# Eight of 160 dense tokens move their down products from the dense blocks to gathered rows, with the gate stage starting three blocks later

## The chip, the cores and the metric

One NeuronCore of one Trainium2 chip runs the whole program in a single launch. The metric is the device time of that launch in microseconds (us); lower is better. All arithmetic that matters here is float32. TensorE is PE in the rows (its weight loads PEld), VectorE is DVE, ScalarE is ACT, GpSimd is POOL, and SyncE is SP.

## The reference, cut to what matters

Two layers; each has a mixer (attention and pooling in layer 0, a gated MLP in layer 1) and then a PEER channel mixer, which takes most of the time. 256 tokens of width 1024 go through it. Per token, 8 heads pick 16 of 16384 one-neuron experts each, so 128 (expert, gate) pairs:

```python
expert = (i1 * PEER_N_KEYS + i2).reshape(T, PEER_HEADS * PEER_TOPK)      # ids, 128 per token
gate = jax.nn.softmax(best, axis=-1).reshape(T, PEER_HEADS * PEER_TOPK)
hid = jax.nn.gelu(jnp.einsum('cd,ckd->ck', xb, w_down[eb]))              # down products of the picked experts
out = jnp.einsum('ck,ckd->cd', (gb * hid), w_up[eb])                     # weighted sum of their up rows
```

`w_down` and `w_up` have 16384 rows of 1024 floats each, 64 MB per layer and table.

## The kernel before, in words

**Two ways of doing a token.** Tokens 0 to 63 (SPARSE) and 64 to 95 (MORE) are done by gathers: an indirect DMA from POOL fetches one row of the table for each of the 128 partitions (512 KB a gather, line 622), and DVE multiplies it with the token's activations and sums (`dots`, line 1580), or adds it with its coefficient to a running sum in the up stage (`axpy`, line 1697). There are 64 + 32 = 96 such gathers of down rows and 96 of up rows a layer. The other 160 tokens (DENSE) go through all experts: for each of 128 blocks of 128 experts, `down(b)` (line 1234) makes 8 matmuls with a 128x128 weight and the 160 token columns; `up` does the same for the up table. Each float32 matmul stands in the trace as two records, so a block has 16 records.

**Order on TensorE, per layer.** Blocks 0 to 76 of the down stage; then the transposes of gates and ids (line 1273, at block IDS_AT = 77); blocks 77 to 79; then 40 turns, each `down(G_FROM + g)` followed by `token_gates(g)` (line 1249), four one-hot matmuls (8 records) for four tokens; then 8 more down blocks; then the 128 up blocks, which begin with the pairs 0 to 7 (two blocks each). Until block G_FROM = 80 ScalarE's Gelu writes the block of activations; from there the block holds ones, gates are multiplied into it, and DVE multiplies the activated products in (`hidden`, line 1680).

**What a turn needs.** For turn g POOL builds two of the four gated one-hots (`build_first`, line 633, two instructions of line 638), DVE the compare for the other two (line 1668), and ACT scales them and builds the second factor (lines 902, 907, 910). PE waits for all three, and for the gates product of turn g-2. DVE's turn is `hidden`, `build_first`, one or two `dots`, `gate` (line 1678). POOL and ACT may run two turns ahead of PE (`g_mm`, line 635).

**POOL's queue.** It is in order. Before the turns it issues the first EARLY + RING - 1 = 49 gathers (line 641), each held until the row five earlier has landed (IN_FLIGHT, line 612) and its ring slot was read. After the build of turn g > 2 it issues what `dots_after(g + G_FROM - 2) + RING - 1` newly permits (line 648). `dots_after` spreads the rows after EARLY = 40 over 44 blocks. The first 40 dots lie between DVE's top-k steps of the second token tile (`early_dot`).

**Loads.** SP and, in part, ACT load the blocks of the tables, eight down blocks ahead; the loads from ALONE_FROM = 80 on are SP's alone. At the end of the down stage SP waits in this order (lines 560 to 565): row 90 of the ring used, load pair 2; pair 4; all rows used, load pair 3 into `spare`, where the activations of MORE lie; pair 6.

Of the kernel before, what the change touches and what calls it, by code (L numbers as in the profile page):

```python
# [15 lines left out]
P = 128  # L16
# [51 lines left out]
GATHERS = 2 * ROWS  # L68
TGROUPS = DENSE // TOK
POOL_TOK = TOK // 2  # L70
# [6 lines left out]
IDS_AT = 77  # L77
# [4 lines left out]
G_FROM = 80  # L82
# [21 lines left out]

def row_of(n):

    if SPARSE_FIRST <= n < EARLY:
        return True, n - SPARSE_FIRST
    if n >= ROWS - MORE_LAST:
        return True, n - PICKS  # L110
    return False, n if n < EARLY else n - MORE + MORE_LAST


def up_row_of(n):

    return (True, n - PICKS) if n >= PICKS else (False, n)


def token_of(g):

    return DENSE_FROM + g * TOK


def ring_uses():

    filled, last, uses = [0] * RING, [None] * RING, []
    for n in range(LAYERS * GATHERS):
        q = n % GATHERS
        slot = q % RING if q < ROWS else (q - ROWS) % UP_RING
# [73 lines left out]
def build_trunk(nc, x_d, consts_d, gfin_d, tab_d, iota_d, lncount_d, poolm_d, poolw_d,  # L203
                pscale_d, wm_d, ws_d, bs_d, cnorm_d, subk_d, wd_d, wu_d, gff_d, sel_d, rows_d, up_rows_d, out_d):
    ctx = ExitStack()
    with ctx:
# [43 lines left out]
        sel = sb("sel", [P, 4 * P + PARTS], F32)  # L250
# [27 lines left out]
        part_of = sel[:, 4 * P:]  # L278
# [66 lines left out]
        def down_psum(s):  # L345
            return ps[:, DOWN_BANKS[s], 0:DENSE]
# [59 lines left out]
        more_rows_sb, more_gates_sb = sem("more_rows_sb"), sem("more_gates_sb")  # L406
        more_ids_psum, more_found_done, more_taken = sem("more_ids_psum"), sem("more_found_done"), sem("more_taken")
# [46 lines left out]
        def _(sp):  # L454
            for l in range(LAYERS):
# [140 lines left out]
        def _(pool):  # L596
            for l in range(LAYERS):
# [10 lines left out]
                def gather(q):  # L608
# [3 lines left out]
                    if IN_FLIGHT <= q < ROWS:  # L612
                        slot, filled, _ = uses[q - IN_FLIGHT + l * GATHERS]
                        pool.wait_ge(row_full[slot], 16 * (filled + 1))
                    table = rows_d if q < ROWS else up_rows_d
                    more, j = row_of(q) if q < ROWS else up_row_of(q - ROWS)
                    if q < ROWS and more and j == 0:
                        pool.wait_ge(more_taken, l + 1)
                    if q < ROWS and not more and j % (PICKS // PIECES) == 0:
                        pool.wait_ge(picks_taken, 2 * (PIECES * l + j // (PICKS // PIECES) + 1))  # L620
                    index = (more_index if more else row_index)[:, j:j + 1]
# [41 lines left out]
        def _(act):  # L663
# [50 lines left out]
            for l in range(LAYERS):  # L714
# [140 lines left out]
                def take_hidden(b):  # L855
                    act.wait_ge(w_used, b + 1 + l * LAYER + MIX_BLOCKS)
                    nc.scalar.activation(block_of(b), down_psum(b % SLOTS), ACT.Gelu_apprx_tanh).then_inc(h_done, 1)  # L857
# [6 lines left out]
                def write_ones(i):  # L864
                    if i == 0:
                        act.wait_ge(h_rows_psum, l + 1)
                        act.wait_ge(more_rows_sb, 16 * PARTS * (l + 1))
                    first = G_FROM * DENSE + i * ONES
# [957 lines left out]
```

## Time and profile before

| | |
|---|---|
| median of three runs | 1514.79 us (1514.16 to 1517.17) |
| the profiled execution | 1503.53 us, its span 1501.7 us |
| granted TensorE clock | 0.997 of full speed |
| PE busy | 1479.2 us, 98% of the span |
| DVE, ACT, POOL busy | 892.0, 473.2, 716.5 us |
| moved by DMA | 523.12 MB, mean 348 GB/s |

The profiled execution is a single one, 11.3 us under the median of the others. A row of the timeline has the start in us, the length in us, engine, line, operation, operands and count; in brackets stands how long the engine was idle before, and what released it. Records of one engine may overlap by their latency, so the pace of a group is read from start to start.

### The profile page before, as it was taken

The page shows a single profiled execution, that of the slowest core. Times are in us where ns is not written, and L with a number is a line of the kernel's source. Part 1 is how long each engine was busy: PE and PEld are TensorE (multiplying, and loading weights), DVE is VectorE, ACT ScalarE, POOL GpSimd, SP SyncE. Part 2 cuts the span into 40 slices and gives each one's busy share as a digit, 9 for nine tenths or more (in the row PEclk, how much of TensorE's full clock was granted, in tenths as well). Part 3 has the DMA queues.
Part 4 walks back from the last instruction along what each step waited for, and adds up shares of the span by engine and source line. Part 5 has one row for each costly group of instructions (what it writes and reads, how often), then busy time and mean ns, then how long its engine had stood idle before and what let it go on. Part 6 is the DMA issues. An engine that isn't in the chain of part 4 may idle for free.

```text
span 1501.7 us, 29008 instructions
## 1 busy us (share of the span) xinstructions
PE 1479.2 (98%) x10648; PEld 1440.7 (96%) x10648; DVE 892.0 (59%) x2921; ACT 473.2 (32%) x1184; POOL 716.5 (48%) x632
## 2 busy tenths in 40 slices
PE   8999999999999999999999999999999999999996
PEld 6889999999999999999978999999999999999996
DVE  1740999948885444444623449997588834444363
ACT  6663231248881000000055533121788500000001
POOL 6577033448994333333467831333699723332350
PEclk9999999999999999999999999999999999999998
DMA  7356999999999999999845679999999999999993
GB/s 257 133 204 235 332 339 364 409 408 342 383 389 407 416 416 417 416 417 415 360 150 200 211 244 351 349 407 408 367 375 385 383 416 415 416 417 416 417 404 141
DMA packets 126416, 523.12 MB, mean 348 GB/s; under 512 B 14816, under 2 KB 15072, under 8 KB 109536
## 3 DMA queue, kind: packets, MB, share of 16 engines
q1 hardware_dynamic: 56896, 240.27, 42.0%
q0 software_dynamic: 55296, 201.35, 34.3%
q10 hardware_dynamic: 14112, 80.04, 13.1%
q8 instruction: 65, 1.06, 0.3%
q14 instruction: 47, 0.39, 0.1%
HBM read 519.48 MB, written 1.05 MB: 347 GB/s over the span
## 4 chain that ended last, share of the span: by engine, by line
PE 94%; POOL 1%; DMA 1%; issue 1%; ACT 1%; DVE 1%; DVEq 0%; POOLq 0%; SPq 0%; ACTq 0%
PE ps L992 93%; POOL w_lo L605 1%; DMA spare<-in_wu 1%; PE ps L1000 1%; ACT hT_hi L707 0%; DMA raw<-in_wm 0%; DMA xs<-in_x 0%; ACT w_hi L692 0%; ACT arena L680 0%; DVE arena L1385 0%; DVE rtmp L1374 0%; DVE arena L1523 0%; POOL arena L630 0%; PE ps L1322 0%; PE ps L1120 0%
## 5 line engine op out<-in xcount | busy, mean ns | idle before, releaser
L992 PE MATMUL ps<-arena,raw 128*128 128x160 f32 (+1 forms) x2688 | 377.4, 299 | 0.2
L992 PE MATMUL ps<-arena,w_raw 128*128 128x160 f32 (+1 forms) x2688 | 377.3, 299 | 0.0
L992 PEld LDWEIGHTS ps<-arena,raw 128*128 128x128 f32 x2688 | 368.1, 190 | 0.7 <-issue 0.7
L992 PEld LDWEIGHTS ps<-arena,w_raw 128*128 128x128 f32 x2688 | 368.2, 190 | 0.0
L622 POOL DMA_INDIRECT arena<-in_up_rows,ret x192 | 188.1, 979 | 355.1 <-DVE oh_buf L1697 263.3
L622 POOL DMA_INDIRECT arena<-in_rows,ret x192 | 200.0, 1042 | 285.8 <-ACT ret L879 104.5
L1697 DVE SCALAR_TENSOR_TENSOR oh_buf<-arena,ret,oh_buf 128x1024 f32<-128x1024 f32 x126 | 161.8, 1284 | 227.9 <-DMA arena<-in_up_rows,ret 227.9
L605 POOL TENSOR_TENSOR w_lo<-raw,w_hi 128x1024 fp32r<-128x1024 f32 x80 | 194.0, 2436 | 90.8 <-PE ps L992 66.1
L992 PE MATMUL ps<-arena 128*128 128x160 f32 (+5 forms) x1336 | 184.5, 302 | 0.4 <-DMA spare<-in_wu 0.3
L992 PEld LDWEIGHTS ps<-arena 128*128 128x128 f32 (+2 forms) x1336 | 177.9, 189 | 4.0 <-issue 2.6
L1580 DVE SCALAR_TENSOR_TENSOR arena<-arena,ps 128x1024 f32<-128x1024 f32 x128 | 153.6, 1213 | 0.0
L969 ACT ACTIVATE arena<-consts 128x768 f32<-128x768 f32 x2 | 1.7, 842 | 450.0 <-PE ps L992 450.0
L638 POOL TENSOR_SCALAR oh_buf<-iota,ret 128x128 f32<-128x128 f32 x160 | 127.0, 802 | 12.7 <-PE ps L992 10.0
L857 ACT ACTIVATE arena<-ps 128x160 f32<-128x160 f32 x160 | 48.6, 304 | 265.9 <-PE ps L992 265.9
L1697 DVE SCALAR_TENSOR_TENSOR ret<-arena,ret 128x1024 f32<-128x1024 f32 x62 | 82.6, 1333 | 69.2 <-DMA arena<-in_up_rows,ret 66.3
L692 ACT ACTIVATE w_hi<-raw 128x1024 fp32r<-128x1024 f32 x80 | 83.5, 1059 | 83.4 <-DMA raw<-in_wm 57.9
L902 ACT ACTIVATE ret<-iota,ret 128x128 f32<-128x128 f32 x320 | 100.8, 386 | 1.4 <-PE ps L992 1.4
L1633 DVE SCALAR_TENSOR_TENSOR arena<-iota,ret,ps 128x54 f32<-128x54 f32 x512 | 99.9, 265 | 0.0
L1580 DVE SCALAR_TENSOR_TENSOR arena<-arena,spare 128x1024 f32<-128x1024 f32 x64 | 76.4, 1217 | 18.5 <-DMA arena<-in_rows,ret 18.5
L1678 DVE TENSOR_TENSOR arena<-arena,ps 128x512 f32<-128x512 f32 x80 | 54.8, 685 | 52.1 <-PE ps L992 52.1
L992 PE MATMUL ps<-oh_buf,ret 128*128 128x128 f32 x640 | 84.6, 275 | 0.6 <-issue 0.6
L992 PE MATMUL ps<-arena,spare 128*128 (+1 forms) x576 | 82.2, 299 | 0.0
(149 smaller groups left out, 1780.6 us busy)
## 6 DMA issues: line engine op xcount, KB each, us to landing
raw<-in_wd SPq DMA_DIRECT2D x92, 512.0 KB, 6.8
w_raw<-in_wd SPq DMA_DIRECT2D x92, 512.0 KB, 7.6
raw<-in_wm SPq DMA_DIRECT2D x80, 512.0 KB, 3.4
low_rows<-in_wu SPq DMA_DIRECT2D x18, 1024.0 KB, 7.9
arena<-in_wu SPq DMA_DIRECT2D x18, 1024.0 KB, 7.9
arena<-in_wd SPq DMA_DIRECT2D x32, 512.0 KB, 4.9
raw<-in_wu SPq DMA_DIRECT2D x14, 1024.0 KB, 8.0
raw<-in_wu ACTq DMA_DIRECT2D x14, 1024.0 KB, 8.0
```

Of the source, the lines that this page charges most:

```text
L605: nc.gpsimd.tensor_tensor(w_lo[:, s % WLO, :], raw[:, s, :], whs[:, s].bitcast(F32), ALU.subtract).then_inc(wlo_pool, 1)
L622: nc.gpsimd.indirect_dma_start(ring[s], None, table, bass.IndirectOffsetOnAxis(ap=index, axis=0)).then_inc(row_full[s], 16)
L638: nc.gpsimd.tensor_scalar(oh1g[:, g % 2, k, :], iota[:, :], i1T[:, t:t + 1], gT[:, t:t + 1], ALU.is_equal, ALU.mult).then_inc(oh1_pool, 1)
L692: nc.scalar.activation(whs[:, s], raw[:, s, :], ACT.Copy).then_inc(whi_done, 1)
L857: nc.scalar.activation(block_of(b), down_psum(b % SLOTS), ACT.Gelu_apprx_tanh).then_inc(h_done, 1)
L902: nc.scalar.activation(oh2[:, g % 2, k, :], iota[:, :], ACT.Abs, scale=-1.0, bias=i2T[:, t:t + 1]).then_inc(oh2_far, 1)
L992: return nc.tensor.matmul(out, lhsT, rhs, start=start, stop=stop, skip_group_check=shared)
L1000: last = nc.tensor.transpose(ps[:, bank + banks[i], o:o + P], src[:, t, c * P:(c + 1) * P], ident[:, :])
L1580: nc.vector.scalar_tensor_tensor(row, row, 1.0, more_rows if more else h_rows, ALU.mult, ALU.mult, accum_out=(more_hid if more else row_hi ...
L1633: step(nc.vector.scalar_tensor_tensor(found[:, (j * 8 + k) % 24, :], places, cif[:, t, n:n + 1], pay[:, h, :], ALU.is_equal, ALU.mult, acc ...
L1678: nc.vector.tensor_tensor(part, part, gates, ALU.mult).then_inc(gmul_done, 1)
L1697: ins = nc.vector.scalar_tensor_tensor(out, row, coef[:, j:j + 1], out, ALU.mult, ALU.add)
```

## The change

MID = 8: the dense tokens 96 to 103 take their down products from eight more gathers a layer (128 partitions = 8 tokens x 16 parts, each with 8 experts), and `down` multiplies 152 columns instead of 160. The up stage keeps its 160 columns: the eight tokens' activations are multiplied into their gates before these are built into one-hots. Their turns are put last (turns 38 and 39), and there the gates product is a copy. IDS_AT goes from 77 to 80 and G_FROM from 80 to 83; there are still 40 turns, and five down blocks after them. The eight rows are rows 44 to 51 of now 104, and the rows after the fortieth are spread over 43 blocks. The row's product has its activations in `spare[:, 1]`, loaded by 16 more small DMAs of SP.

```diff
+MID, MID_TO = 8, DENSE_FROM + 8
+MID_PARTS = P // MID
+DOWN_ROWS = ROWS + MID
+GATHERS = DOWN_ROWS + ROWS
+DOWN_COLS = DENSE - MID
-IDS_AT = 77
+IDS_AT = 80
-G_FROM = 80
+G_FROM = 83
+DOT_BLOCKS = BLOCKS - G_FROM - 2
+MID_FIRST = EARLY + 4
+MID_GELU_AT, MID_SPREAD, MID_TURN = G_FROM + 14, 16, 18
 def dots_after(b):
-    return EARLY + max(0, min(ROWS - EARLY, (b - G_FROM - 1) * (ROWS - EARLY) // 44))
+    return EARLY + max(0, min(DOWN_ROWS - EARLY, (b - G_FROM - 1) * (DOWN_ROWS - EARLY) // DOT_BLOCKS))
...
+                for i in range(MID_PARTS):
+                    sp.dma_start(mid_rows[i * MID:(i + 1) * MID, :],
+                                 gff[DENSE_FROM:MID_TO, :]).then_inc(mid_rows_sb, 16)
...
-                sp.wait_ge(row_used, l * GATHERS + ROWS - ROWS % RING)
+                sp.wait_ge(row_used, l * GATHERS + DOWN_ROWS - DOWN_ROWS % RING)
                 load_up(RING_PAIR, RING_PAIR)
                 load_first(RAW_PAIRS)
-                sp.wait_ge(row_used, l * GATHERS + ROWS)
+                sp.wait_ge(row_used, l * GATHERS + DOWN_ROWS)
+                sp.wait_ge(mid_psum, l + 1)
                 load_up(SPARE_PAIR, SPARE_PAIR)
...
+                    if g == MID_GROUP:
+                        pool.wait_ge(mid_gates_done, l + 1)
...
-                        free = min(ROWS, dots_after(g + G_FROM - 2) + RING - 1)
+                        free = min(DOWN_ROWS, dots_after(g + G_FROM - 2) + RING - 1)
...
+                def activate_mid():
+                    act.wait_ge(row_used, l * GATHERS + MID_FIRST + MID)
+                    nc.scalar.activation(mid_hid, mid_hid, ACT.Gelu_apprx_tanh).then_inc(mid_gelu_done, 1)
...
+                    if with_mid:
+                        pe.wait_ge(mid_spread_done, l + 1)
+                        mm(mid_psum_of(slot), mid_rows[:, 0:P], mid_token).then_inc(mid_psum, 1)
                     out = down_psum(slot)
                     for c in range(DC):
-                        last = mm(out, block_in[:, c * P:(c + 1) * P], hT[:, c, :], c == 0, c == DC - 1)
+                        last = mm(out, block_in[:, c * P:(c + 1) * P], hT[:, c, MID:], c == 0, c == DC - 1)
...
+                pe.wait_ge(mid_of_done, l + 1)
+                mm(ps[:, 5, SEQ:SEQ + P], mid_of, idf[:, 0, :]).then_inc(more_ids_psum, 1)
...
                         nc.vector.scalar_tensor_tensor(
-                            row, row, 1.0, more_rows if more else h_rows, ALU.mult, ALU.mult,
-                            accum_out=(more_hid if more else row_hid)[:, j:j + 1]).then_inc(row_used, 1)
+                            row, row, 1.0, (h_rows, more_rows, mid_rows)[kind], ALU.mult, ALU.mult,
+                            accum_out=(row_hid, more_hid, mid_hid)[kind][:, j:j + 1]).then_inc(row_used, 1)
...
-                step(nc.vector.tensor_copy(gT, ps[:, 5, 0:SEQ]))
+                step(nc.vector.tensor_copy(gT[:, DENSE_FROM:], ps[:, 5, DENSE_FROM:SEQ]))
...
+                    if g < MID_GROUP:
+                        nc.vector.tensor_tensor(part, part, gates, ALU.mult).then_inc(gmul_done, 1)
+                    else:
+                        nc.vector.tensor_copy(part, gates).then_inc(gmul_done, 1)
+
+                def spread_mid():
+                    dve.wait_ge(mid_gelu_done, l + 1)
+                    nc.vector.tensor_tensor(mid_spread, mid_hid.unsqueeze(1).to_broadcast([P, MID_PARTS, MID]),
+                                            mid_part_of.unsqueeze(2).to_broadcast([P, MID_PARTS, MID]),
+                                            ALU.mult).then_inc(mid_spread_done, 1)
+
+                def gate_mid():
+                    b = G_FROM + MID_TURN
+                    dve.wait_ge(h_psum, b - G_FROM + 1 + hiddens_before)
+                    dve.wait_ge(mid_psum, l + 1)
+                    part = gT[:, DENSE_FROM:MID_TO]
+                    nc.vector.tensor_tensor(part, part, mid_psum_of(b % SLOTS), ALU.mult).then_inc(mid_gates_done, 1)
```

## Rows read from the trace of the kernel before

**Rows 1.** The page's part 4, chain by line; part 5, one group of weight loads.
```profile
PE 94%; POOL 1%; DMA 1%; issue 1%; ACT 1%; DVE 1%; DVEq 0%; POOLq 0%; SPq 0%; ACTq 0%
...
L992 PEld LDWEIGHTS ps<-arena,w_raw 128*128 128x128 f32 x2688 | 368.2, 190 | 0.0
```

**Rows 2.** Timeline of PE: a turn of the gate stage, and blocks before up.
```profile
382.01 1.05 PE L992 MATMUL ps<-oh_buf,ret 128*128 128x128 f32 x8
382.90 2.34 PE L992 MATMUL ps<-arena,raw 128*128 128x160 f32 x16
...
1196.70 8.86 PE L992 MATMUL ps<-arena,w_raw 128*128 128x160 f32 x64
1205.39 4.51 PE L992 MATMUL ps<-arena,low_rows 128*128 128x160 f32 x32
```

**Rows 3.** Timeline of POOL in the gate stage of layer 0.
```profile
349.43 1.59 POOL L638 TENSOR_SCALAR oh_buf<-iota,ret 128x128 f32<-128x128 f32 x2 [0.29 <-PE ps L992]
351.19 1.03 POOL L622 DMA_INDIRECT arena<-in_rows,ret  x1 [0.17 <-DVE arena L1580]
352.52 0.94 POOL L622 DMA_INDIRECT arena<-in_rows,ret  x1 [0.30 <-issue]
353.50 1.59 POOL L638 TENSOR_SCALAR oh_buf<-iota,ret 128x128 f32<-128x128 f32 x2
...
356.33 1.59 POOL L638 TENSOR_SCALAR oh_buf<-iota,ret 128x128 f32<-128x128 f32 x2
```

**Rows 4.** Timeline of PE, turn 37 of layer 0.
```profile
447.07 1.13 PE L992 MATMUL ps<-oh_buf,ret 128*128 128x128 f32 x8 [0.28 <-issue]
```

**Rows 5.** Timeline of DVE, a turn with one dot.
```profile
380.03 0.69 DVE L1678 TENSOR_TENSOR arena<-arena,ps 128x512 f32<-128x512 f32 x1 [0.67 <-PE ps L992]
380.64 1.21 DVE L1580 SCALAR_TENSOR_TENSOR arena<-arena,ps 128x1024 f32<-128x1024 f32 x1
...
381.78 0.31 DVE L1684 TENSOR_TENSOR arena<-arena,ps 128x160 f32<-128x160 f32 x1
...
383.10 0.69 DVE L1678 TENSOR_TENSOR arena<-arena,ps 128x512 f32<-128x512 f32 x1 [0.68 <-PE ps L992]
```

**Rows 6.** Timeline of POOL, layer 0: gathers number 26, 44 and 48.
```profile
258.33 0.94 POOL L622 DMA_INDIRECT arena<-in_rows,ret  x1 [1.00 <-DMA arena<-in_rows,ret]
...
317.62 1.30 POOL L622 DMA_INDIRECT arena<-in_rows,ret  x1 [1.55 <-DMA arena<-in_rows,ret]
...
...
328.50 0.94 POOL L622 DMA_INDIRECT arena<-in_rows,ret  x1 [1.61 <-DMA arena<-in_rows,ret]
```

**Rows 7.** Busy time by window; after the engines: clock, DMA share, GB/s.
```profile
270.00:300.00 30.00, 30.00 (x223) 30.00 (x222) 28.45 (x177) 6.83 (x16) 11.76 (x10) 1.00 1.03 409
390.00:420.00 30.00, 30.00 (x238) 30.00 (x237) 26.04 (x54) 25.71 (x81) 27.41 (x32) 1.00 1.00 379
```

**Rows 8.** Timeline of DVE, layer 0: end of top-k, first copy of the gates.
```profile
318.59 0.29 DVE L1647 TENSOR_TENSOR ret<-ret,gsum 128x128 f32<-128x128 f32 x1
324.45 0.42 DVE L1651 COPY ret<-ps 128x256 f32<-128x256 f32 x1 [5.56 <-PE ps L1278]
```

**Rows 9.** Timelines of POOL and DVE near the end of layer 0.
```profile
130.36 2.40 POOL L605 TENSOR_TENSOR w_lo<-raw,w_hi 128x1024 fp32r<-128x1024 f32 x1 [0.48 <-PE ps L992]
...
735.21 5.65 POOL L605 TENSOR_TENSOR w_lo<-raw,w_hi 128x1024 fp32r<-128x1024 f32 x2 [5.60 <-PE ps L992]
...
736.25 7.08 DVE L1697 SCALAR_TENSOR_TENSOR ret<-arena,ret 128x1024 f32<-128x1024 f32 x3 [2.44 <-DMA arena<-in_up_rows,ret]
```

**Rows 10.** SP's timeline, layer 1; issues of 1199 to 1202 (us to landing last).
```profile
1200.31 0.33 SPq L536 DMA_DIRECT2D spare<-in_wu  x1
...
spare<-in_wu SPq DMA_DIRECT2D x1, 1024.0 KB, 10.1
```

**Rows 11.** Timelines of DVE and PE at the end of layer 0.
```profile
747.63 1.28 DVE L1697 SCALAR_TENSOR_TENSOR ret<-arena,ret 128x1024 f32<-128x1024 f32 x1 [0.89 <-DMA arena<-in_up_rows,ret]
...
752.81 1.02 PE L992 MATMUL ps<-oh_buf,sel 128*128 128x512 f32 x2
```

More of the change, by code:

```diff
@@ L92, with column_of @@
 EARLY, EARLY_PLACES = SPARSE_FIRST + MORE - MORE_LAST, 14
+DOT_BLOCKS = BLOCKS - G_FROM - 2
+MID_FIRST = EARLY + 4
+MID_GELU_AT, MID_SPREAD, MID_TURN = G_FROM + 14, 16, 18
 def dots_after(b):
-    return EARLY + max(0, min(ROWS - EARLY, (b - G_FROM - 1) * (ROWS - EARLY) // 44))
+    return EARLY + max(0, min(DOWN_ROWS - EARLY, (b - G_FROM - 1) * (DOWN_ROWS - EARLY) // DOT_BLOCKS))
 def early_after(i):
     return (i + 1) * EARLY // EARLY_PLACES
+ROW, MORE_ROW, MID_ROW = range(3)
 def row_of(n):
[L107 to L111, printed above, removed]
+    if n < SPARSE_FIRST:
+        return ROW, n
+    if n < EARLY:
+        return MORE_ROW, n - SPARSE_FIRST
+    if MID_FIRST <= n < MID_FIRST + MID:
+        return MID_ROW, n - MID_FIRST
+    if n >= DOWN_ROWS - MORE_LAST:
+        return MORE_ROW, n - DOWN_ROWS + MORE
+    return ROW, n - MORE + MORE_LAST - (MID if n >= MID_FIRST else 0)
 def up_row_of(n):
-    return (True, n - PICKS) if n >= PICKS else (False, n)
+    return (MORE_ROW, n - PICKS) if n >= PICKS else (ROW, n)
+def column_of(g):
+    return (MID + g * TOK) % DENSE
 def token_of(g):
-    return DENSE_FROM + g * TOK
+    return DENSE_FROM + column_of(g)
 def ring_uses():
@@ L128, in ring_uses @@
         q = n % GATHERS
-        slot = q % RING if q < ROWS else (q - ROWS) % UP_RING
+        slot = q % RING if q < DOWN_ROWS else (q - DOWN_ROWS) % UP_RING
         uses.append((slot, filled[slot], last[slot]))
@@ L317, in build_trunk @@
         more_found = ret[:, 0:MORE]
+        mid_found = ret[:, MORE:MORE + MID]
+        mid_index = ret[:, MORE + MID:MORE + 2 * MID].bitcast(U32)
+        mid_hid = ret[:, MORE + 2 * MID:MORE + 3 * MID]
+        mid_rows = spare[:, 1, :]
+        mid_spread = mid_rows[:, 0:P].rearrange("p (b j) -> p b j", j=MID)
         spread = ret[:, 2 * SEQ:2 * SEQ + P].rearrange("p (b j) -> p b j", j=MORE)
+        mid_of = ret[:, 2 * SEQ + P:3 * SEQ]
+        mid_ids = mid_of.rearrange("p (b j) -> p b j", j=MID)
         h_rows = ps[:, 2:4, :].rearrange("p b n -> p (b n)")
@@ L611, in gather @@
                         pool.wait_ge(row_used, last + 1)
[L612 removed]
+                    if IN_FLIGHT <= q < DOWN_ROWS:
                         slot, filled, _ = uses[q - IN_FLIGHT + l * GATHERS]
                         pool.wait_ge(row_full[slot], 16 * (filled + 1))
[L615 to L617 removed]
+                    table = rows_d if q < DOWN_ROWS else up_rows_d
+                    kind, j = row_of(q) if q < DOWN_ROWS else up_row_of(q - DOWN_ROWS)
+                    if q < DOWN_ROWS and kind == MORE_ROW and j == 0:
                         pool.wait_ge(more_taken, l + 1)
[L619 removed]
+                    if kind == MID_ROW and j == 0:
+                        pool.wait_ge(mid_taken, l + 1)
+                    if q < DOWN_ROWS and kind == ROW and j % (PICKS // PIECES) == 0:
                         pool.wait_ge(picks_taken, 2 * (PIECES * l + j // (PICKS // PIECES) + 1))
[L621 removed]
+                    index = (row_index, more_index, mid_index)[kind][:, j:j + 1]
                     nc.gpsimd.indirect_dma_start(
@@ L1232, in _, with down @@
                             last.then_inc(sc_psum, 1)
-                def down(b):
+                def down(b, with_mid=False):
                     slot, block_in = b % SLOTS, down_slot(b)
@@ L1283, in _ @@
                 for g in range(TGROUPS):
-                    down(G_FROM + g)
+                    down(G_FROM + g, with_mid=g == MID_TURN)
                     token_gates(g)
@@ L1682, in hidden @@
                     dve.wait_ge(gmul_done, gates + gates_before)
-                    part = block_of(b)
+                    part = hidden_of(b)
                     nc.vector.tensor_tensor(part, part, down_psum(b % SLOTS), ALU.mult).then_inc(hmul_done, 1)
                 def axpy(n):
-                    q = ROWS + n
+                    q = DOWN_ROWS + n
                     wait_row(q)
-                    more, j = up_row_of(n)
+                    kind, j = up_row_of(n)
                     row = ring[uses[q + l * GATHERS][0]]
-                    out, coef = (more_sums, more_coef) if more else (sums, row_coef)
+                    out, coef = (more_sums, more_coef) if kind == MORE_ROW else (sums, row_coef)
                     if j == 0:
@@ L1762, in shape_tables @@
     part = t[:, :PARTS] == p // MORE
-    sel = np.concatenate([more, own, own.T, more.T, part], axis=1).astype(f)
+    mid_part, mid_token = t[:, :MID_PARTS] == p // MID, t[:, :MID] == p % MID
+    sel = np.concatenate([more, own, own.T, more.T, part, mid_part, mid_token], axis=1).astype(f)
     return {"tab": tab, "lncount": lncount, "poolm": poolm, "ident": np.eye(P, dtype=f),
```

57 lines of the change are left out of this document (43 added, 14 removed).

## The prediction

> **What bounds the kernel now.** I read the chain that ended last first. It is PE for 94% of the span [rows 1], so the median moves with what PE does, and an engine beside it counts only where PE would wait for it. Next PE's timeline: four down blocks of 160 columns run from 1196.70 to 1205.39, 8.69 us for 64 records, 135.8 ns a record and 2.173 us a block; eight records of 128 columns take 0.89 us, 111 ns each [rows 2]. A turn of the gate stage is therefore 2.17 + 0.89 = 3.06 us.
>
> Then the engines that feed a turn. **POOL is the one to see.** From its build at 349.43 to that at 353.50 it does a build and two gathers in 4.07 us; from 353.50 to 356.33 a build and one gather in 2.83 us [rows 3]. So one more gather costs 1.24 us, and a build alone about 2.83 - 1.03 - 0.14 = 1.66. After the first of these rows none of its builds waits for PE. Each build may begin when the gates of two turns before are done, which gives it 2 x 3.06 - 0.89 - 1.62 = 3.6 us of lead; in turn 37 that is used up, and PE stands 0.28 us for it [rows 4]. POOL's queue, at 48% of the span on the page, is full in these 40 turns: a share over the span hides that. DVE has 0.68 us to spare in a turn of one dot, and a dot takes 1.14 us from start to start [rows 5].
>
> **What the change takes off.** Eight columns less in each of 128 x 16 down records a layer. Between 160 and 128 columns a record falls by 24.7 ns [rows 2], which would be 6.2 ns for eight columns; the 128-column records come in short groups that may carry something of their own, so I take the pass itself, 135.8 ns x 8/160 = 6.8 at most, and 6.7. A block goes from 2.173 to 2.066 us, a layer by 128 x 0.107 = **13.7 us**; two layers by 27.4. The up stage keeps 160 columns and gains nothing.
>
> The weight loads could forbid this: they fill 368.2 us / 2688 = 137 ns a record, as long as the products [rows 1], yet at 128 columns the pair goes at 111 ns [rows 2], so they stretch and don't bind. The Trainium skill (TensorE: Matmul & The Clock Gate, "LDWEIGHTS (loading the stationary operand)") puts a load at its columns over 1.2 GHz, 107 ns, under the new pitch of 129; by that rule the whole 13.7 us is open too, and the trace agrees in its 111 ns.
>
> **What the gate stage gives back.** A turn of PE would be 2.07 + 0.89 = 2.96 us. POOL's turn gets longer. By the formula of the schedule, up to the build of turn 39, turns 3 to 38 held 44 gathers, one turn none; now 52, again one turn none. POOL's time for those 36 turns:
> - before: 35 x 2.83 + 9 x 1.24 + 1.66 = 111.9 us, against PE's 36 x 3.06 = 110.2. It falls behind by 1.7, plus some 2 us in the first turns when it waits for PE: the lead just goes, as rows 4 show.
> - after: 35 x 2.83 + 17 x 1.24 + 1.66 = 121.8 us, against 36 x 2.96 = 106.6. It falls behind by 15.2 us, 16.6 with the early waits, less a lead of 2 x 2.96 - 0.89 - 1.62 = 3.4: **13.2 us** of standing PE.
> Before it was 0.3, so 12.9 us a layer go back. The mean turn becomes 3.3 us or so, longer than before, though its products are shorter. DVE does not bind: a turn of one dot is 3.07 - 0.68 = 2.39 us [rows 5], and (104 - 40)/43 = 1.49 dots make 2.39 + 0.49 x 1.14 = 2.95, just under 2.96 and well under POOL's 3.3.
>
> **The start of the stage.** Block 83 begins 80 x 0.107 = 8.5 us earlier for the shorter blocks and three blocks of 2.07 later: 2.3 us earlier than block 80 did. POOL's 49th gather does not follow. Between gathers 26 and 44 (18 of them) it needed 59.3 us, 3.29 each, then 10.9 for four, 2.72 each, waiting on rows in flight [rows 6], with the DMA at 409 GB/s [rows 7]. Down blocks take 0.524 MB / 2.173 us = 241 GB/s of that and now 254, which leaves the rows 155 for 168, so 3.57 us each. The faster pace at the end comes when PE reaches the last shared loads, 7.7 us earlier: 51.6 us at 3.57 make 14.5 gathers, the other 7.5 take 20.4, and the last stands at 330.3 instead of 328.50. POOL is 1.8 + 2.3 = 4.1 us later against PE than before. About 2 us of that it had to spare (first build at 329.5, wanted at 332.9, 1.6 long); I take **1.8 us**, bounds 0 and 4.1. At the ids PE came 5.6 us after DVE had finished [rows 8]; it now comes 2 earlier, DVE has some 0.8 us of new small work and rows 2 to 3 us later, so this wait is about nil (0 to 2, inside the same bounds).
>
> **A port between DVE and POOL.** The eight new dots read the row and `spare`, both SBUF, in turns 3 to 11, beside POOL's builds; the dots there so far had one operand in PSUM. Near the end of layer 0, three such two-SBUF operations of DVE took 7.08 us, 1.28 alone [rows 11], and two of POOL's 5.65 us, 2.40 alone [rows 9]: 3.2 us lost on DVE and 0.85 on POOL for three meetings. POOL's share is 0.28 a meeting: 8 x 0.28 = 2.3 less some POOL idle in the early turns, **1.3 us** a layer. Bounds: 0, and a dot of 1.14 each time, 9.1 us. The Trainium skill (SBUF — State Buffer, "Who interferes with whom") says that such a DVE instruction and a GpSimd one that reads SBUF exclude each other for the whole instruction. By that rule the price is anywhere up to the bound, by which comes first; the rows agree that both lose.
>
> **The rest.** On PE one more 128-column matmul before the stage and one of eight columns in it: 2 x 0.11 = **0.2 us**. The id conversions shrink a little, off the path. ACT's three short operations fit in turns in which it waits for POOL anyway, and its Gelu of the new rows comes four turns after the last of them. SP issues 16 small DMAs more after block 0, with eight blocks loaded ahead. **The tail**: five down blocks (10.3 us) for eight before, and eight dots in them; DVE ends the last one about 1.5 us after the up stage begins. Before, `spare`'s pair was issued at 1200.31, 5.1 us ahead of the up stage at 1205.39, and took 10.1 us [rows 2, 10]. It is wanted 6 x 2.17 = 13.0 us into that stage; issued at +1.5 it lands at 11.6 if it takes the same, or at 14 to 16 behind the late pair 4 of the same queue. Up rows also start later, and layer 0 has 752.8 - 748.9 = 3.9 us for that [rows 11]. I take **0.8 us**, bounds 0 and 3.
>
> **The sum**, per layer: -13.7 + 12.9 + 1.8 + 1.3 + 0.2 + 0.8 = +3.3 us; two layers +6.6. The profiled execution of 1503.5 us (span 1501.7) would become 1510.1; it lies 11.3 us under the median, and as the terms are differences I put them on the median: 1514.8 + 6.6 = 1521.4, say 1521.5.
>
> **Rivals.**
> - *POOL gives way (faster).* Its stretch of 0.30 before a second gather may be no work, leaving 0.94 for it, and the queue may run closer to PE. 17 x 0.3 = 5.1 us a layer less, no port, no late start: -13.7 + 7.8 + 0.2 = -5.7, two layers -11.4, 1503.4. If POOL never bound, 1514.8 - 27 = 1488. It decides from the point at which POOL's 36 turns fall under 106.6 + 3.4 + 13 us or so of other cost, that is, at a mean turn under 3.3 us with nothing else late. Against: the gap stands before every second gather, and PE already stood for POOL. Chance 0.17, of it 0.05 near 1488.
> - *Only POOL's queue (no change).* The queue costs as worked out, and start, port and tail hide: -13.7 + 12.9 + 0.2 = -0.6 a layer, up to +1.5 with a part of them: 1513.6 to 1517.8. For: each of these has a bound at nil. Chance 0.25.
> - *The port blocks whole (slower still).* 9.1 for 1.3 us: 1521.5 + 15.6 = 1537. For: rows 9. Against: builds fill half of a turn, so that half of the meetings hit gathers. Chance 0.07.
> - *Weight loads bind and nothing shrinks.* Outside the stage 88 x 0.107 = 9.4 us a layer fail to come: 1521.5 + 19 = 1540. Against: 111 ns. Chance 0.02.
>
> **Numbers.** Forecast 0.49: 1521.5 us, its own range 1518 to 1529. The range that holds 8 in 10 takes in the no-change rival and part of the faster one: 1508 to 1531. Slower by over 0.2% (3 us, about what a measurement can tell from none) 0.49 + 0.07 + 0.02 = 0.58; within 0.25; faster 0.17.
>
> **What the changed profile would show.** Blocks before the stage at 2.07 us. POOL without a gap from turn 7 or so on, and PE standing about 1 us in every second turn from turn 13, the wait naming POOL's build or plain issue; 40 turns in 130 to 134 us, 123 before. Builds in the first ten turns longer than 1.59 for two, or dots on `spare` longer than 1.22, if the port counts. The last down dot after the first up product. The forecast is wrong if turns run at 2.96 us, if a gather after a gather costs under 1 us, or if down blocks stay at 2.17.

## Result and the profile after

The changed kernel takes **1548.16 us** (median of 4 runs, 1547.32 to 1551.47), the kernel before 1514.47 beside it: ratio 1.0224, 95% interval 1.0204 to 1.0243, 34 us slower. Forecast were 1521.5, in 1508 to 1531. The direction held, the size did not.

The profiled execution of the changed kernel took 1547.3 us (span 1545.5), close to its median. That of before was 11 us under its own; a second one of before (below, `e_before`) took 1512.9. So differences against the first profile make 44 us where medians make 34, and I trust them by stretches that repeat.

Which engine sets the end, the page's chain of the changed kernel:
```profile
PE 43%; DMA 25%; DVE 20%; issue 7%; POOL 2%; ACT 2%; DVEq 0%; POOLq 0%; SPq 0%; ACTq 0%
```
PE was 94% of it [rows 1]. Transfers and DVE now hold nearly half of the chain. PE's timeline, first where it comes to the ids, then in the gate stage, then at the stage's end:
```profile
316.39 8.43 PE L1048 MATMUL ps<-arena,w_raw 128*128 128x152 f32 x64
...
327.86 0.69 PE L1336 MATMUL ps<-consts,ret 128*128 128x128 f32 x2 [3.04 <-DVE ret L1718]
328.34 0.63 PE L1339 MATMUL ps<-consts,ret 128*128 128x128 f32 x2
328.77 9.68 PE L1048 MATMUL ps<-arena,raw 128*128 128x152 f32 x64
339.40 1.13 PE L1048 MATMUL ps<-oh_buf,ret 128*128 128x128 f32 x8 [0.96 <-ACT ret L964]
...
382.73 2.23 PE L1048 MATMUL ps<-arena,raw 128*128 128x152 f32 x16
385.68 1.13 PE L1048 MATMUL ps<-oh_buf,ret 128*128 128x128 f32 x8 [0.72 <-issue]
386.64 2.23 PE L1048 MATMUL ps<-arena,raw 128*128 128x152 f32 x16
388.71 1.05 PE L1048 MATMUL ps<-oh_buf,ret 128*128 128x128 f32 x8
...
476.14 1.13 PE L1048 MATMUL ps<-oh_buf,ret 128*128 128x128 f32 x8 [1.77 <-issue]
...
775.10 2.08 PE L1048 MATMUL ps<-oh_buf,sel 128*128 128x512 f32 x2 [5.00 <-DVE ret L1785]
```
A block is what was forecast: 64 records in 8.27 us from start to start (1063.36 to 1071.63), 2.067 us a block. All else is what stands between blocks. PE stands 3.04 us for top-k's end, and then its next records are slow: 9.68 us for 64. The windows around it say why (time, PE busy, granted clock, DMA share, GB/s):
```profile
324.00:327.00 3.00, 0.83 (x7) 1.00 1.03 412
328.00:331.00 3.00, 3.00 (x13) 0.50 1.03 410
331.00:334.00 3.00, 3.00 (x24) 0.95 1.03 407
```
The granted clock was 1.00 before the stand and 0.50 behind it: 13 records in 3 us, 24 in the next 3. The stand costs itself and some 2 us more (1.25 in the 64 records, 0.5 in the transposes before them), and the first gates then wait 0.96 us for ACT. The prediction had no term for that.

In the stage POOL has no gap, and PE stands 0.7 us in every second turn, as foreseen. What was foreseen in kind and priced too low: POOL's own instructions get longer. POOL's builds of turns 6 to 9 with the gathers between them, and the changed kernel's DVE beside the first of them:
```profile
352.48 1.59 POOL L682 TENSOR_SCALAR oh_buf<-iota,ret 128x128 f32<-128x128 f32 x2 [0.18 <-issue]
...
356.54 2.59 POOL L682 TENSOR_SCALAR oh_buf<-iota,ret 128x128 f32<-128x128 f32 x2
359.30 1.76 POOL L664 DMA_INDIRECT arena<-in_rows,ret  x1 [0.17 <-issue]
361.10 3.24 POOL L682 TENSOR_SCALAR oh_buf<-iota,ret 128x128 f32<-128x128 f32 x2
...
366.80 3.29 POOL L682 TENSOR_SCALAR oh_buf<-iota,ret 128x128 f32<-128x128 f32 x2
```
```profile
354.71 1.21 DVE L1648 SCALAR_TENSOR_TENSOR arena<-arena,ps 128x1024 f32<-128x1024 f32 x1
...
356.45 1.22 DVE L1648 SCALAR_TENSOR_TENSOR arena<-arena,spare 128x1024 f32<-128x1024 f32 x1
...
358.94 1.22 DVE L1648 SCALAR_TENSOR_TENSOR arena<-arena,spare 128x1024 f32<-128x1024 f32 x1
```
The dots on `spare` take 1.22 us, as those on PSUM do (among the others of these turns is one of 1.51); POOL pays.

At the end of the layer the rows are late. Windows of DVE's busy time, clock, share and GB/s, inside the gate stage and the up stage, first of before, then of after:
```profile
345.00:460.00 115.00, 100.16 (x209) 1.00 1.00 378
500.00:740.00 240.00, 108.41 (x84) 1.00 1.02 416
```
```profile
345.00:460.00 115.00, 95.59 (x194) 1.00 0.95 351
500.00:740.00 240.00, 100.50 (x79) 1.00 1.02 416
```
**This is the view that I had not read.** From 500 us on the DMA moves 416 GB/s in both kernels, window by window: it is full in the up stage before the change already. The changed kernel has eight rows of 0.524 MB more in a layer, 4.2 MB or 10.1 us at that rate. Where do they go? The windows from the first gates to behind the last, and from there to the product that collects the rows' sums (PE busy, clock, share, GB/s), first of before, then of after:
```profile
332.94:454.17 121.23, 120.95 (x946) 1.00 0.98 374
454.17:752.81 298.64, 298.39 (x2200) 1.00 0.99 405
```
```profile
339.40:477.10 137.70, 120.92 (x946) 1.00 0.95 351
477.10:775.10 298.00, 292.00 (x2152) 1.00 1.00 403
```
Rate times length: the longer gate stage takes 48.3 MB for 45.3, and the stretch behind it 120.1 MB for 120.9, about as many as before, while PE has 7 us less to do in it. So the added bytes do not pile up there; it is PE that now comes earlier to rows that come as before. The last row has landed by 768.6 us (the DMA view from there on lists no packet of the rows' queue), and PE is ready at 770.10. What it then waits for is DVE, which does its last nine rows in one piece of 16.21 us, too late to wait for any of them, beside POOL's last gather and two `w_lo`:
```profile
756.93 1.28 DVE L1785 SCALAR_TENSOR_TENSOR ret<-arena,ret 128x1024 f32<-128x1024 f32 x1 [2.16 <-DMA arena<-in_up_rows,ret]
758.83 16.21 DVE L1785 SCALAR_TENSOR_TENSOR ret<-arena,ret 128x1024 f32<-128x1024 f32 x9 [0.62 <-DMA arena<-in_up_rows,ret]
```
```profile
762.35 6.07 POOL L645 TENSOR_TENSOR w_lo<-raw,w_hi 128x1024 fp32r<-128x1024 f32 x2
```
Narrower windows of DVE divide the piece: seven of the nine take 1.28 us, and the two beside the `w_lo` take
```profile
763.00 3.20 DVE L1785 SCALAR_TENSOR_TENSOR ret<-arena,ret 128x1024 f32<-128x1024 f32 x1
...
766.30 3.19 DVE L1785 SCALAR_TENSOR_TENSOR ret<-arena,ret 128x1024 f32<-128x1024 f32 x1
```
That is 3.8 of the 5.0 us for which PE waits. Before the change the same meeting took 2.40 and 3.17 us (the first two adds of the three in [rows 9]) and cost PE nothing:
```profile
736.25 2.40 DVE L1697 SCALAR_TENSOR_TENSOR ret<-arena,ret 128x1024 f32<-128x1024 f32 x1 [2.44 <-DMA arena<-in_up_rows,ret]
...
738.77 3.17 DVE L1697 SCALAR_TENSOR_TENSOR ret<-arena,ret 128x1024 f32<-128x1024 f32 x1
```

I cut the layers into three stretches by PE's timeline: A, from the first down product to the first gates (layer 0); B, from there to the first down product behind the last gates (layers 0 and 1); C, from there to the first product that collects the rows' sums (both layers). "Less x" is the difference of the ratios to before, times 1513 us; each is uncertain by some 5 us. Against `e_before`, whose execution lies close to the median, the 34 us of after lie almost all in B: 16.7 and 16.4, with -2.7 in A of layer 0.

| kernel | ratio to before | A | B | C |
|---|---|---|---|---|
| before | 1 | 178.4 | 121.2, 121.2 | 298.6, 298.8 |
| e_before | (one execution, 1512.9 us) | 185.1 | 121.0, 121.1 | 298.7, 298.3 |
| after | 1.0224 | 182.4 | 137.7, 137.5 | 298.0, 297.6 |
| e_spread | 1.0219 | 182.3 | 139.6, 137.7 | 297.4, 297.3 |
| e_port | 1.0159 | 181.9 | 132.5, 130.9 | 299.0, 297.1 |
| e_both | 1.0143 | 182.2 | 130.9, 130.8 | 297.8, 296.0 |
| e_early | 1.0195 | 182.7 | 132.2, 132.1 | 298.9, 299.1 |
| e_wide | 1.0265 | 185.2 | 137.5, 137.6 | 299.1, 298.5 |
| e_pool1 | 1.0052 | 181.3 | 123.4, 123.0 | 299.1, 300.9 |
| e_up8 | 1.0122 | 180.6 | 137.7, 137.7 | 291.9, 291.7 |
| e_less | 1.0058 | 181.1 | 122.7, 122.9 | 298.7, 295.7 |
| e_pool1_up8 | 0.9956 | 182.3 | 124.1, 125.4 | 291.7, 293.6 |
| e_before_pool1 | 0.9968 | 179.1 | 120.5, 120.6 | 298.5, 298.3 |

PE's own products would make after's A 176.2, B 116.3, C 291.5 (298.6 less 8 x 2.173 plus 5 x 2.067). So 6.2, 21.4 and 6.5 us a layer stand in between.

### The profile page after: what moved, and what is told of

It is laid out like the page before. It is cut to its first block, busy times and chain, and to the rows that moved or that the text cites. A ratio compares the mean times of both kernels' runs of the same rounds, so it can differ in the third digit from the quotient of the medians.

```text
span 1545.5 us, 29128 instructions
## 1 busy us (share of the span) xinstructions
PE 1473.5 (95%) x10656; PEld 1424.6 (92%) x10656; DVE 913.0 (59%) x2957; ACT 472.9 (31%) x1184; POOL 746.1 (48%) x648
## 3 DMA queue, kind: packets, MB, share of 16 engines
q10 hardware_dynamic: 14112, 80.04, 12.7%
## 4 chain that ended last, share of the span: by engine, by line
PE 43%; DMA 25%; DVE 20%; issue 7%; POOL 2%; ACT 2%; DVEq 0%; POOLq 0%; SPq 0%; ACTq 0%
PE ps L1048 43%; DMA arena<-in_up_rows,ret 16%; DMA arena<-in_rows,ret 7%; DVE arena L1648 4%; DVE arena L1704 4%; DVE oh_buf L1609 2%; DVE oh_buf L1606 2%; POOL w_lo L645 2%; DVE arena L1613 2%; DVE ret L1785 1%; DVE arena L1751 1%; DVE ret L1609 1%; DMA raw<-in_wm 1%; DVE oh_buf L1785 1%; DMA spare<-in_wu 1%
## 5 line engine op out<-in xcount | busy, mean ns | idle before, releaser
L1048 PE MATMUL ps<-arena,raw 128*128 128x152 f32 (+2 forms) x2688 | 368.4, 296 | 0.0
L1048 PE MATMUL ps<-arena,w_raw 128*128 128x152 f32 (+2 forms) x2688 | 367.4, 296 | 1.0 <-DVE arena L1772 0.8
L664 POOL DMA_INDIRECT arena<-in_rows,ret x208 | 215.5, 1036 | 302.7 <-ACT ret L924 101.0
L1048 PEld LDWEIGHTS ps<-arena,raw 128*128 128x128 f32 x2688 | 360.4, 192 | 0.0
L1048 PEld LDWEIGHTS ps<-arena,w_raw 128*128 128x128 f32 x2688 | 358.4, 191 | 2.0 <-issue 1.9
L1048 PE MATMUL ps<-arena 128*128 128x152 f32 (+6 forms) x1336 | 183.5, 301 | 3.2 <-issue 2.5
L682 POOL TENSOR_SCALAR oh_buf<-iota,ret 128x128 f32<-128x128 f32 x160 | 140.3, 884 | 8.7 <-PE ps L1048 5.2
L901 ACT ACTIVATE arena<-ps 128x152 f32<-128x152 f32 x166 | 49.0, 296 | 252.9 <-PE ps L1048 232.3
L1048 PEld LDWEIGHTS ps<-oh_buf,ret 128*128 128x128 f32 x640 | 78.7, 192 | 40.2 <-issue 33.6
L1648 DVE SCALAR_TENSOR_TENSOR arena<-arena,spare 128x1024 f32<-128x1024 f32 x80 | 97.0, 1230 | 25.1 <-DMA arena<-in_rows,ret 25.1
```

Source lines behind the costliest of these rows:

```text
L664: nc.gpsimd.indirect_dma_start(ring[s], None, table, bass.IndirectOffsetOnAxis(ap=index, axis=0)).then_inc(row_full[s], 16)
L682: nc.gpsimd.tensor_scalar(oh1g[:, g % 2, k, :], iota[:, :], i1T[:, t:t + 1], gT[:, t:t + 1], ALU.is_equal, ALU.mult).then_inc(oh1_pool, 1)
L901: nc.scalar.activation(hidden_of(b), down_psum(b % SLOTS), ACT.Gelu_apprx_tanh).then_inc(h_done, 1)
L1048: return nc.tensor.matmul(out, lhsT, rhs, start=start, stop=stop, skip_group_check=shared)
L1648: nc.vector.scalar_tensor_tensor(row, row, 1.0, (h_rows, more_rows, mid_rows)[kind], ALU.mult, ALU.mult, accum_out=(row_hid, more_hid, mid ...
```

## Experiments

**A second profile of before.**

> The kernel before, unchanged, for a second profile: the first one was taken from an execution 11 us under the median. If its stages in this profile are as long as in the first (gate stage of 40 turns 123.4 us in layer 0), the stage rows of before stand, and only some waits differ; if the stage is longer by several us, the differences by stage have to be taken against this profile. Expected: stages within 1 us, total near 1514.

B and C are as in the first profile. A is 6.6 us longer: around 205 to 210 us PE stands 2.5 us in pieces, DVE too, with no engine to wait for, and from 208.7 us on PE's granted clock is 0.50 for 6.8 us. Such gaps come in some executions of either kernel (DVE has 1.9 us of them in the profile of after). The last line is a window of PE, with busy time, clock, share and GB/s:
```profile
208.73 0.08 DVE L1633 DVE_READ_ACCUMULATOR arena<-iota,ret,ps 128x1 f32 x1 [0.77 <-issue]
208.76 0.89 PE L992 MATMUL ps<-arena,w_raw 128*128 128x160 f32 x2 [0.88 <-issue]
...
208.70:215.50 6.80, 6.21 (x21) 0.50 1.04 411
```

So my first profile was a quick execution of before, and its stretch A is a bad measure for others.

**The small loads spread.** My first theory of the late top-k: SP issues the 16 loads of `spare` in one piece of 10.87 us (161.90 to 172.77), the down loads of blocks 16 to 23 wait behind them.
```diff
-                for i in range(MID_PARTS):
+                def spread_rows(i):
                     sp.dma_start(mid_rows[i * MID:(i + 1) * MID, :],
                                  gff[DENSE_FROM:MID_TO, :]).then_inc(mid_rows_sb, 16)
...
                         load_down(WIDE + j, j % DOWN_RAW)
+                    if j < MID_PARTS:
+                        spread_rows(j)
```
(and ONES_FROM 20 for 12)

> The changed kernel, with the 16 small loads into `spare` issued one after each of SP's next 16 down loads instead of all at once, and ACT's ones from block 20 on. Theory of the blocked queue (SP stands 10.9 us for them, the down loads of blocks 16 to 23 come late, the backlog takes the DMA from the rows, top-k ends late, PE stands 3.0 and 3.7 us at the ids and 2.3 us more at the first gates): these waits fall to under 1 us a layer, the kernel comes 8 to 12 us under the changed one, at 1536 to 1540. Rival, the late start is due to the order of the stage itself (rows later against PE as the prediction summed it, 1.8 us a layer) or to the mixer before it: less than 3 us in all.

Ratio 1.0219 (1.0191 to 1.0248), 1 us less, with stands of 3.10 and 4.36 us at the ids (the difference is within the uncertainty). The theory fell. The blocked queue is there but is made up for before the rows need the DMA. The rival's size fell too (A 6 us over PE's own). Where DVE's time goes: from its first work on the scores to top-k's end in layer 0 it had 167.0 us before, 173.5 after, and its waits for rows in the second half grew from 9.1 to 12.3 us, in this kernel 12.7; some 1.1 us are new small operations, 1 to 2 us are gaps as above.

**The mid dots against PSUM.**
```diff
-                            row, row, 1.0, (h_rows, more_rows, mid_rows)[kind], ALU.mult, ALU.mult,
+                            row, row, 1.0, (h_rows, more_rows, h_rows)[kind], ALU.mult, ALU.mult,
```

> The changed kernel, with the dots of the eight mid rows against `h_rows` (PSUM) in place of their copy in `spare` (SBUF): the down products of these eight tokens are then other numbers, the work is the same. Theory of the port: POOL's pairs of builds beside these dots (2.4 to 3.3 us, 1.59 alone) all take 1.59 again, the gate stage of 40 turns falls from 140.7 to 133 or so, and the kernel comes 12 to 16 us under the changed one, at 1532 to 1536. Rival, POOL's queue alone sets the stage and the long builds are spent in its slack: the stage loses under 2 us a layer, the kernel under 4. The wait at the ids stays at 3 to 4 us.

Ratio 1.0159 (1.0129 to 1.0189), 10 us less, short of the 12 to 16 expected and above the rival's 4; the stage 132.5 and 130.9 for 137.7. (The eight tokens' products are other numbers in this kernel and the next; the work is the same.) POOL in the same turns:
```profile
352.27 1.59 POOL L682 TENSOR_SCALAR oh_buf<-iota,ret 128x128 f32<-128x128 f32 x2 [0.18 <-issue]
...
356.33 1.59 POOL L682 TENSOR_SCALAR oh_buf<-iota,ret 128x128 f32<-128x128 f32 x2
358.08 1.03 POOL L664 DMA_INDIRECT arena<-in_rows,ret  x1 [0.16 <-issue]
359.15 1.58 POOL L682 TENSOR_SCALAR oh_buf<-iota,ret 128x128 f32<-128x128 f32 x2
```
The stretched builds are gone with the second SBUF operand of DVE and nothing else: **5 to 7 us a layer are the port in the gate stage**, POOL's queue is the other 15 or so. The two stretched adds at the layer's end are in this kernel too (3.20 and 3.19 us, PE waits 6.79 us there).

**Both edits.**

> Both edits, spread loads and mid dots against `h_rows` (same note on the eight tokens' products). If the two causes are separate, their gains add: 20 to 28 us under the changed kernel, 1521 to 1527, which is what the prediction's sum gave with its own bounds for the port and the start. If they overlap (an earlier start only gives POOL more to wait for), the sum is short by over 5 us.

Ratio 1.0143 (1.0119 to 1.0168), 12 us less and not 20: the port's part alone. Still 23 us over before.

**Mid rows early.** The eight rows go among the 40 of top-k, eight others into the stage.
```diff
-SPARSE_FIRST, MORE_LAST = 18, 10
-EARLY, EARLY_PLACES = SPARSE_FIRST + MORE - MORE_LAST, 14
+SPARSE_FIRST, MORE_LAST = 12, 12
+EARLY, EARLY_PLACES = SPARSE_FIRST + MORE - MORE_LAST + MID, 14
...
-MID_FIRST = EARLY + 4
+MID_FIRST = EARLY - MID
```
(with the spread loads, and `row_of` to fit)

> The changed kernel with spread loads, and the eight mid rows taken among the 40 early rows (in top-k, before the gate stage) in place of eight others, which move into the stage. Same work, same count of dots in each stretch; but no dot on two SBUF operands stands beside POOL's builds in turns 3 to 11. Theory of the port: as good as the dots against `h_rows`, that is 10 to 14 us under the changed kernel, ratio 1.014 to 1.016. Rival, early mid dots cost as much beside the gathers in top-k (the stand at the ids grows from 3 to over 6 us): no gain.

Between the two: 1.0195 (1.0168 to 1.0222). The stage falls to 132.2, as with PSUM, by another way to the same effect; but PE stands 6.79 us at the ids in layer 1, and 4 us of gain are left, which is within the uncertainty.

**What the shorter products were worth.**
```diff
-            return ps[:, DOWN_BANKS[s], 0:DOWN_COLS]
+            return ps[:, DOWN_BANKS[s], MID:DENSE]
...
-                    out = down_psum(slot)
+                    out = ps[:, DOWN_BANKS[slot], 0:DENSE]
...
-                        last = mm(out, block_in[:, c * P:(c + 1) * P], hT[:, c, MID:], c == 0, c == DC - 1)
+                        last = mm(out, block_in[:, c * P:(c + 1) * P], hT[:, c, :], c == 0, c == DC - 1)
```

> The changed kernel, with the down products over all 160 columns again (the first eight are computed and not read), everything else of the change kept. It asks what the 13.7 us a layer of shorter products were worth. Theory: they were worth little, because PE is held in each stage by something else: at the ids by the rows (PE would come 80 x 0.107 = 8.5 us later, the stand of 3 to 4 us goes, and with it 2 us at half clock), in the gate stage by POOL's queue, in the tail by the transfers of the up rows. Then it is 4 to 12 us slower than the changed kernel, ratio to before 1.025 to 1.030. Rival, the prediction's sum, in which outside the gate stage 88 x 0.107 = 9.4 us a layer come through: 19 us slower than the changed kernel, ratio 1.035.

Ratio 1.0265 (1.0235 to 1.0295): with 27.4 us more of products the kernel is **6 us** slower, give or take 5. PE in its stage:
```profile
444.12 1.13 PE L1048 MATMUL ps<-oh_buf,ret 128*128 128x128 f32 x8 [0.54 <-issue]
...
451.02 1.13 PE L1048 MATMUL ps<-oh_buf,ret 128*128 128x128 f32 x8 [0.54 <-issue]
```
Two turns take 6.90 us here, 6.88 in the changed kernel (385.68 to 392.56); only the stand differs, 0.54 for 0.72. At the ids PE does not stand at all, in B nothing changes, in C 1 us. So the change gave up eight rows' worth of POOL, DVE and DMA for products that PE had little use for.

**POOL builds one one-hot** of a turn, DVE compares three, ACT scales three.
```diff
-POOL_TOK = TOK // 2
+POOL_TOK = 1
```

> The changed kernel, with POOL building one one-hot of a turn in place of two; DVE compares three and ACT scales three. Theory, POOL's queue and its port set the gate stage: POOL's turn loses 0.8 us, the stage of 40 turns falls from 137.9 to 120 to 126 (PE alone 116.5, then DVE or ACT bind at about 3.05), the kernel comes 20 to 30 us under the changed one, ratio to before about 1.005 to 1.010. Rival, the transfers of the rows set the stage and not POOL: the stage stays above 133 and POOL waits for rows.

Ratio 1.0052 (1.0029 to 1.0075), **26 us less**, B 123.2. POOL's queue (with the port inside it) was the largest cause: the same edit takes 5 us off the kernel before (`e_before_pool1` below), so some 21 of the 34 us of loss go with it. POOL is busy 85.0 of 115 us in the stage where it was 102.4, and the freed queue lets the rows out, in windows of DVE as above:
```profile
345.00:460.00 115.00, 110.08 (x218) 1.00 1.00 391
```
391 GB/s for 351. C has grown by 1 and 3 us: of 29 us gained in B, 4 come back there.

**Eight up rows less.**
```diff
-GATHERS = DOWN_ROWS + ROWS
+UP_ROWS = ROWS - 8
+GATHERS = DOWN_ROWS + UP_ROWS
...
-                for n in range(ROWS):
+                for n in range(UP_ROWS):
```

> The changed kernel, with the last eight up rows of each layer left out (neither gathered nor added, so the sparse tokens' up products are incomplete): 4.2 MB a layer less, 10 us of transfers at 416 GB/s, all of it behind the gate stage. Theory, from the last gates on it is the transfers that bind (298.5 us before, 297.8 after, though PE has 7 us less to do; the wait of 5.0 us at the layer's end names DVE's last rows): this stretch falls by the 5.0 us of wait plus about 1.5 us at half clock in layer 0 and by 1 to 3 in layer 1, total 6 to 10 us less, ratio about 1.017. Rival, PE's own order sets the stretch and the late row is DVE's speed: under 3 us.

Ratio 1.0122 (1.0096 to 1.0149), 15 us less. C falls by 6 us in each layer, to 291.9 and 291.7, which is PE's own 291.5, and PE waits for no row:
```profile
765.09 1.02 PE L1049 MATMUL ps<-oh_buf,sel 128*128 128x512 f32 x2
```
Layer 1 lost as much as layer 0, though its waits showed 3.4 us only; PE also stood there in gaps with no releaser (0.78, 0.62 and 0.74 us from 1499 on) and at 0.71 of its clock from 1500 to 1505, and with fewer rows that went too. The other 3 us lie in A and the mixer and are within the uncertainty. The edit takes away with the 4.2 MB also eight adds of DVE, 1.28 us each, and eight issues of POOL a layer, and in layer 0 DVE is now through with its rows at 757.37, 7.7 us ahead of PE, the two adds beside `w_lo` still 2.82 and 3.19 us long. So it shows that eight rows a layer are the excess of C, and does not divide this between their transfers and DVE's adds.

**Both of the last two.**

> The changed kernel with POOL's one one-hot and without the last eight up rows of each layer (the sparse tokens' up products are incomplete), so that it moves as many rows as the kernel before. Theory of the transfers: the 4.2 MB a layer are what is left of the loss; 2 x 6 us less than with POOL's one-hot alone, 1508 to 1511, ratio 0.996 to 0.999. If POOL's edit had already taken the load off the tail: 1516 or more.

Ratio 0.9956 (0.9938 to 0.9974), 14.5 us under `e_pool1`; C 291.7 and 293.6. The kernel to set beside it is `e_before_pool1` below, which has the same edit of POOL and as many rows: 1504.07 and 1506.95 us, ratios 0.9956 and 0.9968. So with as many rows as before and POOL relieved the 27 us of shorter blocks bring 2 to 3 us, hardly more than a measurement can tell. That kernel leaves products out, so it is no candidate; it shows that eight rows a layer are what is left of the loss (13 us from `e_before_pool1` to `e_pool1`).

**All that helped, together.** POOL_TOK = 1, mid rows early, spread loads, and 38 early rows; against `e_early` the second edit is
```diff
-SPARSE_FIRST, MORE_LAST = 12, 12
+SPARSE_FIRST, MORE_LAST = 10, 12
```

> The changed kernel with everything that helped put together: POOL builds one one-hot of a turn, the mid rows are early rows, the small loads are spread, and 38 rows in place of 40 are taken in top-k, so that top-k ends some 7 us earlier and PE no longer stands at the ids. By single causes: 1521.9 of POOL's one-hot less 2 x 3 of the stand, less 2 x 2 at half clock, less the port of the early turns (3 or so): 1509 to 1512, under the kernel before. Rival, by now the transfers of a layer bind (404 to 408 GB/s in the gate stage with one one-hot, 416 after it): what is gained ahead of the stage comes back as a wait for the last up rows and for `spare`, and the time stays within 4 us of 1522.

Ratio 1.0058 (1.0037 to 1.0080): no better than POOL's edit alone. The wait at the ids shrank to 1.56 us in layer 0 and was 4.89 in layer 1 (why two rows less did not end top-k earlier I have not found). At the layer's end PE waits 6.11 us for DVE's last row all the same:
```profile
757.40 2.08 PE L1050 MATMUL ps<-oh_buf,sel 128*128 128x512 f32 x2 [6.11 <-DVE ret L1787]
```
The time is the rival's, its mechanism only in part: DVE is through with its last nine rows, gapless and with two adds of 3.19 us among them, 6.7 us after the last packet of a row (750.7). So what was gained ahead came back at the end, but as a backlog of DVE; and as top-k was only partly mended, the run does not settle the rival alone.

**POOL's edit on the kernel before.** `POOL_TOK = 1` again.

> The kernel before, with POOL building one one-hot of a turn. Its gate stage of 121.4 us stood 0.3 us for POOL, and PE's own products take 39 x 3.06 + 1.1 = 120.4: a gain of at most 0.5 us a layer, ratio 0.999 to 1.001, or a loss of a few us if DVE (0.68 us to spare in a turn of one dot, none in one of two) is late with three compares. If it gained over 5 us, POOL's queue had bound the kernel before as well, and the account of the change would be wrong.

Ratio 0.9968 (0.9951 to 0.9985), 1506.95 us: **faster than both kernels**, by 0.3%, a complete kernel. Its B shows 0.6 to 0.7 us a layer of it, the last stands for POOL; the rest of the 4.8 I can't place, and the interval reaches down to 2.3. The expectation (at most 0.5 us a layer) was missed, and its bar of 5 us, over which POOL's queue would have bound the kernel before as well, lies inside the interval. In B it did not bind by more than 0.7 us a layer.

## Why the prediction failed, step by step

Per layer the forecast was +3.3 us, and the medians give 17. By the stretches B was to be 116.3 + 13.2 + 1.3 = 130.8 and came to 137.6, and C was to be 291.5 + 0.8 = 292.3 and came to 297.8. These two stretches are 12 of the 14 us missed. The terms that failed in them are the port, put at 1.3, and the tail, put at 0.8; the queue came out 1 to 3 us over its 13.2.

- *Blocks, -13.7 us a layer*: right as a duration (2.067 us). As a gain it was wrong: by `e_wide` it brought 3 us a layer (0.5 to 6). The sum subtracted it whole and then added what gave it back too low.
- *POOL's queue, +12.9*: right in mechanism, nearly in size. Without the port B is 131 to 132.5 where 116.3 + 13.2 = 129.5 was forecast.
- *The port, +1.3, bound 9.1*: 5 to 7. The step that failed took POOL's share, 0.28 a meeting, from the end of the layer [rows 9], where DVE bore most of it; it counted three meetings where the single adds show two (2.40, 3.17, and 1.28 us). In the gate stage DVE loses next to nothing and POOL 0.9 to 1.7 us in each stretched pair of builds. That is near the rule of the Trainium skill (SBUF — State Buffer, "Who interferes with whom") by which a DVE instruction with two SBUF inputs contends with a GpSimd one that reads SBUF. The trace agrees. By that rule alone the price was anywhere up to the bound of 9.1; the measured one is 5 to 7.
- *The late start, +1.8, bounds 0 and 4.1*: 6.2 in A of layer 0. I had rows 2 to 3 us later and called the wait at the ids nil, measured from an execution in which DVE had 5.6 us to spare. Rows were 3.2 us later, new operations took 1.1 and gaps 1.9, PE came earlier as said; 3.0 us of stand. Then the clock, which I had left out: 2 us at 1.2 GHz behind the stand, and 1.0 for ACT's one-hots. The upper bound had no clock in it. How much of the 6.2 is the change's is open: the second profile of before has 6.6 us over the first in this stretch, by gaps and a slow clock without a stand at the ids.
- *The 16 small loads at nothing*: right in the end, by `e_spread`, though SP was blocked 10.9 us.
- *The tail, +0.8, bounds 0 and 3*: 6.5. The term looked at `spare` and at the last rows' slack of 3.9 us [rows 11], and not at the rows as a stream: with the DMA full (416 GB/s before and after) they end about as late as before (the last packet of a row 293.0 us into C of layer 0 before, 291.4 after), while PE's own products shrink by 7 us. Then the slack is gone, and what stood behind it shows: in layer 0 a wait of 5.0 us for DVE's last adds, 3.8 of it the two that met `w_lo`, a meeting that [rows 9] already held; in layer 1 3.4 us of gaps that name no releaser and a half clock of 3.4 us behind them. `e_up8` shows that eight rows a layer less remove all of it; whether by their bytes or by DVE's adds is not shown.

By stretches, a layer gets -2.2 + 6.2 = +4.0 in A, -4.9 + 21.4 = +16.5 in B, -7.1 + 6.5 = -0.6 in C: 20 us, two layers 40, where the profiles differ by 44 and the medians by 34. Against the second profile of before A falls out of it (-2.7), and B alone makes 33. Of the rivals, *the port blocks whole* (1537) had the mechanism closest to what was seen; its price for the port, 9.1, was too high, and it had the same blank for the tail. *Weight loads bind* (1540) is refuted by the 2.067 us.

## What to carry to other kernels

Before an engine's instructions are made shorter, ask in each stretch who is next: here rows at the ids, POOL in the stage, and behind it the rows with the DMA and DVE, each with 0 to 6 us behind PE, so that 27 us of PE's work were worth 6. Sum the bytes of a stretch against its rate: here C has 120 MB, 289 us at 416 GB/s, beside 291.5 us of PE's own after the change. PE's 7 us less use up the slack that hid what follows the last row, DVE's adds. A row of 0.5 MB is 1.26 us at that rate; eight of them measured 6 to 7 us a layer. And a stand of PE of some 3 us may bring a half clock behind it, 2 us here, which belongs in the upper bound.

## What the runs showed of the hardware that I had not expected

- PE stood 3.04, 3.73 and (in `e_pool1`) 2.81 us at the ids, and its clock was at 1.2 GHz just after each (64 records 9.68, 10.58 and 9.67 us; 8.43 at 2.4 GHz). The length of the stand alone does not decide it: after 3.10 us in `e_spread` the clock stayed at 2.4 (the next 64 records took 8.43), and after 1.35 and 2.61 in `e_up8` too. Of two equal stands of 2.56 us in the gate stage of after, the one in layer 0 left the clock as it was, the one in layer 1 was followed by half clock for 3.4 us. In `e_before` the clock fell amid gaps of 0.3 to 0.9 us. What decides between them no run here shows.
- A DVE dot with two SBUF operands mostly kept its 1.22 us (one in these turns took 1.51) and stretched two POOL builds from 1.59 to 3.29 us, a gather's issue from 1.03 to 1.76. At the end of the layer it was DVE that paid: its adds beside `w_lo` took up to 3.20 us for 1.28, and two `w_lo` 6.07 for 2 x 2.40.
- PE and DVE both stand for 0.2 to 1.0 us at a time with nothing in the profile to wait for, in stretches where the DMA is full (414 GB/s from 205 to 211 us in `e_before`, 414 from 1499 to 1502 in the profile of after); `e_up8`, with fewer rows, has none of them at the end of layer 1. What they are is open.
- SP takes 0.68 us for each load of 32 KB that goes from `arena` to eight partitions of `spare`:
```profile
161.90 10.87 SPq L562 DMA_DIRECT2D spare<-arena  x16
```
